# Modulation units into six places, the input projection's weights behind them in four transfers, bias lines inside its first tile

## The chip, the cores and the metric

One core of one Trainium2 chip runs the program. The metric is the device time of one execution in microseconds (us); smaller is better. Its engines are named as in the profile: PE (TensorE matmul) and PEld (its weight load), DVE (VectorE), ACT (ScalarE), POOL (GpSimd) and SP, which here only issues transfers. "SPq" and "POOLq" are the transfer queues fed by these engines. "Clock" is TensorE's granted clock, where 1.00 is 2.4 GHz and 0.50 is 1.2 GHz.

## The reference, cut to what matters

```python
def reference(...):                       # one decoder layer, prompt group (512 tokens) and 8 samples
    sh_m, sc_m, g_m, sh_f, sc_f, g_f = split(silu(c) @ w_ada + b_ada, 6)     # w_ada: 1024 x 6144
    h = rms_norm(x, norm_mix) * (1 + sc_m) + sh_m
    q, k, v, u = split(h @ w_in)                                             # w_in: 1024 x 1280
    attn = window_attention(rms(q), rms(k), v, bias=rel_bias[bucket(distance)], sinks)
    pool = pooling_mixer(u)
    x = x + g_m * (concat(attn, pool) @ w_out)
    h = rms_norm(x, norm_ffn) * (1 + sc_f) + sh_f
    return x + g_f * moe(h)               # top 4 of 32 experts, w1: 32 x 1024 x 2048, w2: 32 x 1024 x 1024
```

## The kernel before, in words

The program has two parts. `head` computes everything up to the router; `experts` streams the 32 experts' weights (402 MB in f32) through a ring of places in SBUF and multiplies with them. A barrier lies between the two. Every engine's instructions are written out by hand in program order and joined by semaphores. The change touches `head` only, nearly all of it in its first fifth.

**Modulation.** `w_ada` is cut into 24 units of 1 MB (512 rows by 512 columns). Chunk `c` of 512 outputs consists of units `2c` and `2c+1`. SP's `load_ada(n)` loads unit `n` into one of three places (`n % ADA_SLOTS`, in `m.raw`) and first waits until the unit that lay there has been used. PE's `ada(n)` multiplies it (L1349), four column groups at once. When both units of a chunk are done, DVE's `mod_row(c)` adds the bias `bada` and the four groups into `mrow` (L1025, then three times L1029). For chunks 0 to 3 (shift and scale of the mixer, units 0 to 7) PE's `turn_mod(c)` turns the row into columns (L1370). After chunk 3 DVE copies these into `modT` (L1067), forms `g1T` (L1070) and applies them to the normed and turned `hT`, one of eight row blocks `k` at a time (L1079). Chunks 4 to 11 follow between the steps of the attention.

**x.** Five row tiles (four of 128 prompt rows, one of 8 samples) are loaded by SP between the first three units, normed by ACT (L817, L821, L824), turned by PE (L1362) and copied into `hT` by ACT (L830) and DVE (L1045). PE's order is `ada(t)`, `turn_x(t)` for t = 0 to 4 (with `turn_mod(0)` before the last), `ada(5)`, `turn_mod(1)`.

**Bias lines.** For each of the eight heads a matmul of the replicated table `relrep` (33 rows, made by DVE at L1055) with `oh_line` gives a line of 383 values in all partitions (L1387). DVE copies it into `m.line` (L1061). One more matmul of 129 columns gives the samples' bias (L1389, copied at L1063). PE computes the lines after `turn_mod(1)` and before `turn_mod(2)`, `ada(6)`, `ada(7)`, `turn_mod(3)`. POOL stores the lines to HBM (`skew`) and reads them back skewed as `bias`, needed by the first scores.

**Input projection.** `w_in` (5 MB) is one transfer, which SP issues after unit 7. PE's loop over five row tiles multiplies, for each of eight `k`, 512 and 256 columns (L1435, L1436). It waits for `w_in`, for the lines, and in tile 0 for each `h_ready`. Tile t's results are normed by ACT and DVE while PE goes on with tile t+1 and then turns them (`turn_qk`). The sample tile (L1424), the four `u` blocks (L1447), the attention, output projection and router follow.

SP's queue order before is: units 0, 1, 2 each followed by an x tile, the last two x tiles, the first bias row, units 3 to 6 each when its place is free, the second bias row (after chunk 1 is added), unit 7, `w_in`, unit 8 and so on.

Of the kernel before, what the change touches and what calls it, by code (L numbers as in the profile page):

```python
# [21 lines left out]
P = 128  # L22
# [19 lines left out]
ADA_SLOTS = 3  # L42
# [83 lines left out]
def build(nc, i, o):  # L126
    m = Record()
    m.i, m.o = i, o
    with ExitStack() as ctx:
# [86 lines left out]

        m.xs = at("xs", [P, TT, D], F32, H0)
# [34 lines left out]
        m.nf = at("nf", [9, D], F32, H0 + 97792)  # L252
        m.mrow = at("mrow", [9, 2, 512], F32, H0 + 101888)
# [108 lines left out]
def head(nc, m):  # L362
# [16 lines left out]
    s.gate_step = signal("gate_step")  # L379
# [7 lines left out]
    s.win_in = signal("win_in")  # L387
# [19 lines left out]
    s.g1_ready = signal("g1_ready")  # L407
    s.hT_half = signal("hT_half")
# [17 lines left out]
    s.qn_raw = signal("qn_raw")  # L426
# [13 lines left out]
    s.spool_step = signal("spool_step")  # L440
# [24 lines left out]
    s.s_soft = signal("s_soft")  # L465
# [36 lines left out]
    ada_in = [signal(f"ada_in{n}") for n in range(ADA_SLOTS)]  # L502
# [7 lines left out]
    WHOLE = 8  # L510
    ada_bank = [bank[2 + c % 2] if c < 4 else bank[2] for c in range(CHUNKS)]
# [27 lines left out]
    with nc.Block() as block:  # L539

        @block.sync
        def _(sp):
# [7 lines left out]
            def load_ada(n):  # L550
                c, half = n // 2, n % 2
                if n >= ADA_SLOTS:
                    sp.wait_ge(s.ada_used, n - ADA_SLOTS + 1)
                src = i["w_ada"][0, half * 512:(half + 1) * 512, c * 512:(c + 1) * 512]
                sp.dma_start(m.raw[:, n % ADA_SLOTS, :].rearrange("p (k n) -> p k n", k=4),
                             src.rearrange("(k p) n -> p k n", p=P)).then_inc(ada_in[n % ADA_SLOTS], 16)

            def load_bada(q):
                sp.dma_start(m.bada[:], i["b_ada"][0:1, q * D:(q + 1) * D].to_broadcast([9, D])
                             ).then_inc(s.bada_in, 16)  # L560
# [7 lines left out]

            for n in range(ADA_SLOTS):
                load_ada(n)  # L570
                load_x(n)
            for t in range(ADA_SLOTS, TT):
                load_x(t)
            sp.wait_ge(s.c_tr, 1)
            load_bada(0)
            for n in range(ADA_SLOTS, ADA):
                load_ada(n)
                if n == 7:
                    sp.dma_start(m.w_in[:], i["w_in"][0].rearrange("(k p) n -> p k n", p=P)).then_inc(s.win_in, 16)
                if n % 4 == 2:  # L580
                    sp.wait_ge(s.mr_ready, n // 2 - 1)
                    load_bada(n // 4)
                if n in (12, 14, 16, 18):
                    if n == 12:
                        sp.wait_ge(s.z_ready, TT)
                        sp.wait_ge(s.u_ready, 4)
                    k = n - 12
                    sp.dma_start(m.w_out[:, k:k + 2, :],
                                 i["w_out"][0, k * P:(k + 2) * P, :].rearrange("(k p) n -> p k n", p=P)
                                 ).then_inc(s.wout_in, 16)  # L590
                if n >= 14 and n % 2 == 0:
                    store_mod(n // 2 - 3)
# [50 lines left out]
        def _(gp):  # L643
# [30 lines left out]
            gp.wait_ge(s.win_in, 16)  # L674
# [102 lines left out]
            gates = [0]  # L777

            def gate_step(ins):

                ins.then_inc(s.gate_step, 1)
                gates[0] += 1
                gp.wait_ge(s.gate_step, gates[0])
# [19 lines left out]
        def _(act):  # L803
# [34 lines left out]

            act.wait_ge(s.bb_in, 32)
# [162 lines left out]
        def _(v):  # L1002
# [13 lines left out]
            def mod_row(c):  # L1016

                v.wait_ge(s.ada_used, 2 * c + 2)
                v.wait_ge(s.bada_in, 16 * (c // 2 + 1))
# [5 lines left out]
                added = v.tensor_tensor(m.mrow[:, c % 2, :], ada_bank[c][0:9, :], m.bada[:, c % 2 * 512:c % 2 * 512 + 512],  # L1025
                                        ALU.add)
# [30 lines left out]
            for h in range(NH):  # L1057
                v.wait_ge(s.line_tr, h + 1)
                if not h:
                    v.wait_ge(s.c_tr, 1)  # L1060
# [9 lines left out]
            v.scalar_tensor_tensor(m.g1T[:], m.modT[:, 8:16, :], 1.0,  # L1070
                                   m.vecsT[:, 0:8].unsqueeze(2).to_broadcast([P, 8, 9]),
                                   ALU.add, ALU.mult).then_inc(s.g1_ready, 1)
            v.wait_ge(s.g1_ready, 1)
            v.wait_ge(s.xT_act, TT)
            v.wait_ge(s.xT_dve, TT)
            v.tensor_tensor(m.hT[:, :, SEQ:TOK], m.hT[:, :, SEQ:TOK], m.g1T[:, :, 0:NS],
                            ALU.mult).then_inc(s.hT_half, 1)
# [3 lines left out]
            v.wait_ge(s.hT_half, 1)  # L1081
            v.tensor_tensor(m.hT[:, :, SEQ:TOK], m.hT[:, :, SEQ:TOK], m.modT[:, 0:8, 0:NS],
                            ALU.add).then_inc(s.h_ready, 1)

# [8 lines left out]
            for t in range(TT):  # L1093
# [11 lines left out]
                if t:  # L1105
# [3 lines left out]
                                m.hrs[0:R, 0:NH].unsqueeze(2).to_broadcast([R, NH, HD]), ALU.mult).then_inc(s.qn_raw, 1)  # L1109
# [3 lines left out]
                v.wait_ge(s.qn_raw, t + 1)  # L1113
# [3 lines left out]
                v.wait_ge(s.kn_raw, 2 * t + 1)  # L1117
# [15 lines left out]
            for g, w in enumerate(WINDOWS):  # L1133
                v.tensor_reduce(m.dTs[:, g, :], m.spT[:, g, :, BUF + 1 - w:], AX_X, ALU.add).then_inc(s.spool_step, 1)
            v.wait_ge(s.spool_step, 4)
            v.wait_ge(s.Us_ready, 1)
            v.tensor_tensor(m.dTs[:], m.dTs[:], m.Us[:], ALU.add).then_inc(s.spool_step, 1)
            v.wait_ge(s.spool_step, 5)
# [81 lines left out]
            def sample_softmax():  # L1220
                v.wait_ge(s.s_tr, 1)
                v.wait_ge(s.bias64_ready, 1)
                v.scalar_tensor_tensor(m.P64[:], bank[3][0:64, 0:P], HD ** -0.5, m.bias64[:, 0:P], ALU.mult,
                                       ALU.add).then_inc(s.s_soft, 1)
                v.wait_ge(s.s_soft, 1)
                v.tensor_reduce(m.s64[:, 0:1], m.P64[:], AX_X, ALU.max).then_inc(s.s_soft, 1)
                v.wait_ge(s.s_soft, 2)
# [5 lines left out]
                v.tensor_tensor(m.s64[:, 2:3], m.s64[:, 2:3], m.s64[:, 3:4], ALU.add).then_inc(s.s_soft, 1)  # L1233
                v.wait_ge(s.s_soft, 3)
                v.reciprocal(m.s64[:, 4:5], m.s64[:, 2:3]).then_inc(s.s_soft, 1)
                v.wait_ge(s.s_soft, 4)
# [92 lines left out]
        def _(pe):  # L1329
# [10 lines left out]
            def ada(n):  # L1340

                c, half = n // 2, n % 2
                pe.wait_ge(ada_in[n % ADA_SLOTS], 16 * (n // ADA_SLOTS + 1))
# [4 lines left out]
                for k in range(4):  # L1348
                    last = mm(ada_bank[c][32 * k:32 * k + 9, :], m.cT[:, 4 * half + k, :],  # L1349
                              m.raw[:, n % ADA_SLOTS, k * 512:(k + 1) * 512], start=half == 0, stop=half == 1)  # L1350
# [38 lines left out]
            mm(bank[6][0:64, 0:P + 1], m.rel64[:].rearrange("p b h -> p (b h)"), m.oh_s[:], start=True,  # L1389
               stop=True).then_inc(s.bias64_tr, 1)  # L1390
            turn_mod(2)
            ada(6)
            ada(7)
            turn_mod(3)
# [17 lines left out]
            pe.wait_ge(s.win_in, 16)  # L1412
            pe.wait_ge(s.bias64_ready, 1)
# [1242 lines left out]
```

## Time and profile before

| | us |
|---|---|
| median of 3 runs | 1425.12 |
| lowest, highest | 1419.0, 1425.48 |
| the profiled execution | 1425.26 |
| its span in the profile | 1423.7 |
| mean granted clock | 0.92 |

| engine | busy us | share |
|---|---|---|
| PE | 1239.1 | 87% |
| DVE | 668.5 | 47% |
| ACT | 490.2 | 34% |
| POOL | 216.3 | 15% |

The program's two parts have different limits, so these shares say little of the stretch that is changed. That stretch is the first 110 us, and it is read from the timeline there.

### The profile page before, as it was taken

What the parts mean: (1) busy time and instruction counts of PE and PEld (TensorE: products, weight loads), DVE (VectorE), ACT (ScalarE), POOL (GpSimd) and SP (SyncE); (2) the same over time, 40 slices, a digit from 0 to 9 for tenths busy, and PEclk for the clock granted to TensorE, in tenths of its full rate; (3) what the DMA queues carried; (4) which work ended last, traced back from release to release, by engine and by line L of the source; (5) the groups of instructions that cost most, each with busy time, mean ns of one, the idle gap of its engine ahead of it and who ended that gap; (6) DMA issues with size and microseconds to landing.
All of it is one profiled execution on the core that took longest, in us unless ns stands there. A gap on an engine that the chain in (4) does not pass through costs nothing.

```text
span 1423.7 us, 17364 instructions
## 1 busy us (share of the span) xinstructions
PE 1239.1 (87%) x6405; PEld 729.7 (51%) x6405; DVE 668.5 (47%) x969; ACT 490.2 (34%) x703; POOL 216.3 (15%) x285
## 2 busy tenths in 40 slices
PE   5798777986899998899899969999879999999771
PEld 2353435542267564666575427556447555647330
DVE  2531562355378564353585225427334435848313
ACT  5010431231156443233464213225323333727310
POOL 2211321021101111110211102011201021101001
PEclk9799878996999999899999999999989999999975
DMA  9940585438889999999999999999999999999994
GB/s 289 383 119 5 192 286 201 173 128 324 334 309 390 375 403 397 392 396 355 376 411 406 403 391 396 395 354 405 404 388 405 367 346 408 407 410 405 413 393 187
DMA packets 113657, 481.23 MB, mean 338 GB/s; under 512 B 12497, under 2 KB 13824, under 8 KB 83820
## 3 DMA queue, kind: packets, MB, share of 16 engines
q1 hardware_dynamic: 100460, 451.52, 80.3%
q0 software_dynamic: 12768, 27.47, 7.3%
q8 instruction: 52, 0.85, 0.2%
q10 hardware_dynamic: 344, 1.12, 0.2%
q14 instruction: 33, 0.27, 0.0%
HBM read 463.46 MB, written 24.14 MB: 343 GB/s over the span
## 4 chain that ended last, share of the span: by engine, by line
PE 51%; DMA 13%; SPq 5%; DVE 5%; issue 2%; ACT 1%; POOLq 0%; DVEq 0%; ACTq 0%
PE bank L2305 49%; DMA raw<-in_w 10%; SPq L525 3%; DVE rawr L2138 1%; PE bank L2354 1%; DMA yd<-ost,slot_tok 1%; DMA yd<-gu,slot_tok 1%; SPq L531 1%; PE bank L2331 1%; ACT hi L1958 1%; SPq L535 1%; DVE gu L2102 1%; DVE gu L2100 0%; DVE yf L2298 0%; DVE yf L2295 0%
## 5 line engine op out<-in xcount | busy, mean ns | idle before, releaser
L2138 DVE TENSOR_TENSOR rawr<-raw,hi 128x1024 fp32r<-128x1024 f32 x288 | 341.2, 1220 | 137.7 <-ACT hi L1958 134.7
L1958 ACT CAST hi<-raw 128x1024 fp32r<-128x1024 f32 x288 | 295.2, 1049 | 167.0 <-PE bank L2305 117.5
L2305 PE MATMUL bank<-raw,xT_even 128*64 128x512 f32 (+1 forms) x704 | 139.5, 615 | 4.9 <-DMA raw<-in_w 4.9
L2305 PE MATMUL bank<-raw,aT 128*32 128x256 f32 (+1 forms) x992 | 116.4, 485 | 15.4 <-DMA raw<-in_w 15.4
L1853 POOL DMA_INDIRECT yd<-ost,slot_tok x31 | 54.4, 1754 | 356.3 <-ACT ost L1941 356.0
L2305 PE MATMUL bank<-raw,xT_odd 128*32 128x512 f32 (+1 forms) x544 | 88.6, 677 | 21.5 <-DMA raw<-in_w 21.5
L2305 PE MATMUL bank<-hi,xTh_even 128*128 128x512 f32 x256 | 85.1, 415 | 7.5 <-DVE rawr L2138 7.5
L2305 PE MATMUL bank<-hi,aTh 128*128 128x512 f32 x240 | 77.5, 405 | 9.7 <-DVE rawr L2138 9.7
L2305 PEld LDWEIGHTS bank<-raw,aT 128*32 128x32 f32 (+1 forms) x992 | 42.3, 126 | 79.3 <-issue 41.7
L2305 PE MATMUL bank<-rawr,xTh_even 128*128 128x512 f32 x256 | 81.7, 401 | 0.0
L2305 PE MATMUL bank<-hi,xTl_even 128*128 128x512 f32 x256 | 81.2, 399 | 0.0
L2305 PE MATMUL bank<-hi,xTh_odd 128*128 128x512 f32 x224 | 73.2, 408 | 7.0 <-DVE rawr L2138 7.0
L2305 PE MATMUL bank<-rawr,aTh 128*128 128x512 f32 x240 | 76.0, 399 | 0.0
L2305 PE MATMUL bank<-hi,aTl 128*128 128x512 f32 x240 | 75.6, 397 | 0.0
L1926 ACT ACTIVATE gu<-gu 128x512 f32<-128x512 f32 (+1 forms) x50 | 29.1, 583 | 134.9 <-DVE gu L2100 134.9
L2100 DVE TENSOR_SCALAR gu<-bank 128x512 f32<-128x512 f32 (+1 forms) x50 | 31.3, 627 | 94.0 <-PE bank L2305 94.0
L2305 PEld LDWEIGHTS bank<-raw,xT_even 128*64 128x64 f32 (+1 forms) x704 | 35.7, 128 | 69.7 <-issue 58.9
L2305 PE MATMUL bank<-rawr,xTh_odd 128*128 128x512 f32 x224 | 70.2, 395 | 0.0
L2305 PE MATMUL bank<-hi,xTl_odd 128*128 128x512 f32 x224 | 69.9, 394 | 0.0
L2156 DVE SCALAR_TENSOR_TENSOR aTl<-bank,aTh 128x512 fp32r<-128x512 f32 x30 | 20.7, 689 | 100.6 <-ACT aTh L1919 100.6
L1941 ACT ACTIVATE ost<-bank,slot_gate 128x512 f32<-128x512 f32 (+1 forms) x43 | 26.0, 633 | 120.9 <-PE bank L2305 107.6
L2089 DVE TENSOR_REDUCE slot_raw<-bank 128x1 f32<-128x2 f32 (+1 forms) x32 | 5.0, 156 | 126.4 <-PE bank L2305 125.4
(358 smaller groups left out, 1730.1 us busy)
## 6 DMA issues: line engine op xcount, KB each, us to landing
raw<-in_w SPq DMA_DIRECT2D x356, 1024.0 KB, 17.4
raw<-in_w_ada SPq DMA_DIRECT2D x24, 1024.0 KB, 6.0
raw<-in_w SPq DMA_DIRECT2D x48, 512.0 KB, 11.5
w_in_sb<-in_w_in SPq DMA_DIRECT2D x1, 5120.0 KB
w_out_sb<-in_w_out SPq DMA_DIRECT2D x4, 1024.0 KB, 6.2
early<-in_w SPq DMA_DIRECT2D x4, 1024.0 KB, 8.3
xs<-in_x_prompt SPq DMA_DIRECT2D x4, 512.0 KB, 15.7
yd<-zero POOLq DMA_DIRECT2D x4, 512.0 KB, 10.9
```

The costliest lines, as they stand in the source:

```text
L525: sp.dma_start(raw.rearrange("p (k n) -> p k n", k=2), src).then_inc(landed, 16)
L531: sp.dma_start(raw[:, kk * D:(kk + 1) * D].rearrange("p (h c) -> p h c", h=2), src[:, :, j * 512:(j + 1) * 512]).then_inc(landed, 16)
L535: sp.dma_start(raw, src).then_inc(landed, 16)
L1853: gp.indirect_dma_start(yd_of[n], bass.IndirectOffsetOnAxis(ap=m.slot_tok[:, p % 6, b:b + 1], axis=0), out_rows(p, b), None, bounds_check= ...
L1926: nc.scalar.activation(gate, gate, ACT.Silu, scale=ALPHA).then_inc(silu_ready, 1)
L1941: done = nc.scalar.activation(out_rows(p, b)[:, n * w:(n + 1) * w], src, ACT.Copy, scale=m.slot_gate[:, p % 6, b:b + 1])
L1958: nc.scalar.copy(m.hi[:, (2 * n + h) % HI, :], m.raw[:, slot, h * D:(h + 1) * D]).then_inc(hi_done, 1)
L2100: v.tensor_scalar(gate, g, LIMIT, None, ALU.min).then_inc(gmin_ready, 1)
L2102: v.tensor_scalar(up, u, LIMIT, -LIMIT, ALU.min, ALU.max).then_inc(gu_free, 1)
L2138: v.tensor_tensor(m.rawr[slot][:, half], m.raw[:, slot, half], m.hi[:, (2 * n + h) % HI, :].bitcast(F32), ALU.subtract).then_inc(lo_done, 1)
L2156: v.scalar_tensor_tensor(m.aTl[:, k:k + n, :].rearrange("p k n -> p (k n)"), bank[7][:, 0:n * P], 1.0 / ALPHA, m.aTh[:, k:k + n, :].bitcas ...
L2305: return nc.tensor.matmul(out, lhsT, rhs, start=start, stop=stop, skip_group_check=True)
```

## The change

- There are six places for modulation units. Units 0 to 5 go to places 0 to 5 (the three new ones lie in parts of SBUF that are used later); from unit 6 on the first three places are used in turn. SP issues units 0 to 4 each before its x tile, then unit 5, both bias rows (the second into a tile of its own), units 6 and 7, `w_in` in four transfers of 1.25 MB, each with its own semaphore, and unit 8.
- PE runs `ada(6)`, `turn_mod(2)`, `ada(7)`, `turn_mod(3)` right after `turn_mod(1)`. The lines are computed inside tile 0 of the projection, two before each pair of `k`, into banks 6 and 7. The samples' bias is computed before tile 1, which waits for its copy.
- DVE copies two lines after every second `k` of L1079. The two steps for the samples' part of `hT` now follow the eight `k`, and the copy of the samples' bias follows them.
- POOL waits for all four parts of `w_in` before it loads `bb`. ACT waits for chunk 3 before it writes `bb_hi`, which shares space with a new place.
- Several semaphores of DVE and POOL are merged. The four reductions for the samples' pooling now wait one for another, and `qn` and `kn` share a semaphore.

```diff
+        m.ada_more = [at(f"ada_more{n}", [P, 2048], F32, H0 + place) for n, place in enumerate((81216, 89600, 41216))]
+    def ada_place(n):
+        late = ADA_SLOTS + ADA_MORE
+        return n if n < late else (n - late) % ADA_SLOTS
...
-            for n in range(ADA_SLOTS):
-                load_ada(n)
-                load_x(n)
-            for t in range(ADA_SLOTS, TT):
+            for t in range(TT):
+                load_ada(t)
                 load_x(t)
+            load_ada(TT)
             sp.wait_ge(s.c_tr, 1)
             load_bada(0)
-            for n in range(ADA_SLOTS, ADA):
+            load_bada(1)
+            for n in range(TT + 1, WHOLE):
                 load_ada(n)
-                if n == 7:
-                    sp.dma_start(m.w_in[:], i["w_in"][0].rearrange("(k p) n -> p k n", p=P)).then_inc(s.win_in, 16)
+            for n in range(4):
+                sp.dma_start(m.w_in[:, 2 * n:2 * n + 2, :],
+                             i["w_in"][0, 2 * n * P:(2 * n + 2) * P, :].rearrange("(k p) n -> p k n", p=P)
+                             ).then_inc(win_in[n], 16)
+            for n in range(WHOLE, ADA):
+                load_ada(n)
...
+            act.wait_ge(s.ada_used, WHOLE)
+            act.wait_ge(s.mr_ready, WHOLE // 2)
             act.wait_ge(s.bb_in, 32)
...
             mod_row(2)
-            for h in range(NH):
-                v.wait_ge(s.line_tr, h + 1)
...
-                v.tensor_copy(m.line[:, h, :], bank[4 + h % 2][:, 0:LINE]).then_inc(s.line_ready, 1)
-            v.wait_ge(s.bias64_tr, 1)
-            v.tensor_copy(m.bias64[:], bank[6][0:64, 0:P + 1]).then_inc(s.bias64_ready, 1)
             mod_row(3)
...
             for k in range(KC):
                 v.tensor_scalar(m.hT[:, k, 0:SEQ], m.hT[:, k, 0:SEQ], m.g1T[:, k, 8:9], m.modT[:, k, 8:9],
                                 ALU.mult, ALU.add).then_inc(s.h_ready, 1)
+                if k % 2:
+                    for h in (k - 1, k):
+                        v.wait_ge(s.line_tr, h + 1)
+                        v.tensor_copy(m.line[:, h, :], bank[6 + h % 2][:, 0:LINE]).then_inc(s.line_ready, 1)
...
             for g, w in enumerate(WINDOWS):
-                v.tensor_reduce(m.dTs[:, g, :], m.spT[:, g, :, BUF + 1 - w:], AX_X, ALU.add).then_inc(s.spool_step, 1)
+                step(v.tensor_reduce(m.dTs[:, g, :], m.spT[:, g, :, BUF + 1 - w:], AX_X, ALU.add))
...
-            pe.wait_ge(s.rel_ready, 1)
-            for h in range(NH):
+            ada(6)
+            turn_mod(2)
+            ada(7)
+            turn_mod(3)
+            def bias_line(h):
                 if h >= 2:
                     pe.wait_ge(s.line_ready, h - 1)
-                mm(bank[4 + h % 2][:, 0:LINE], m.relrep[:, h, :], m.oh_line[:, 0:LINE], start=True,
+                mm(bank[6 + h % 2][:, 0:LINE], m.relrep[:, h, :], m.oh_line[:, 0:LINE], start=True,
                    stop=True).then_inc(s.line_tr, 1)
...
+            pe.wait_ge(s.rel_ready, 1)
+            pe.wait_ge(s.modT_ready, 1)
             for t in range(TT):
...
                 if t == 1:
-                    pe.wait_ge(s.modT_ready, 1)
+                    pe.wait_ge(s.line_ready, NH)
+                    mm(bank[6][0:64, 0:P + 1], m.rel64[:].rearrange("p b h -> p (b h)"), m.oh_s[:], start=True,
+                       stop=True).then_inc(s.bias64_tr, 1)
+                    pe.wait_ge(s.bias64_ready, 1)
...
                 for k in range(KC):
                     if not t:
+                        if not k % 2:
+                            bias_line(k)
+                            bias_line(k + 1)
+                        pe.wait_ge(win_in[k // 2], 16)
                         pe.wait_ge(s.h_ready, k + 1)
```

## Rows read from the trace of the kernel before

**Rows 1.** The page: granted clock and DMA share in tenths, 40 slices of the span.

```profile
PEclk9799878996999999899999999999989999999975
DMA  9940585438889999999999999999999999999994
```

**Rows 2.** Timeline to 58 us: start, us, engine, line, what; idle before.

```profile
4.97 1.80 SPq L548 DMA_DIRECT2D xs<-in_x_prompt  x2
...
25.86 1.06 ACT L817 ACTIVATE xn<-xs 128x1024 f32<-128x1024 f32 x1
...
16.84 7.80 SPq L555 DMA_DIRECT2D raw<-in_w_ada  x2
...
35.38 0.67 DVE L1055 COPY relrep<-relb 33x1024 f32<-33x1024 f32 x1
...
36.11 1.55 PE L1387 MATMUL bank<-oh_line_sb,relrep 33*128 33x383 f32 x4 [0.40 <-DVE relrep L1055]
...
37.93 2.12 DVE L1029 TENSOR_TENSOR mrow<-mrow,bank 9x512 f32<-9x512 f32 x3
...
43.64 0.56 DVE L1061 COPY line<-bank 128x383 f32<-128x383 f32 x1 [0.72 <-PE bank L1387]
...
48.64 0.69 PE L1389 MATMUL bank<-oh_s_sb,rel 33*64 33x129 f32 x2
...
49.37 0.28 DVE L1063 COPY bias<-bank 64x129 f32<-64x129 f32 x1
...
49.78 3.16 PE L1349 MATMUL bank<-raw,cT 128*9 128x512 f32 x16
...
53.02 0.68 DVE L1025 TENSOR_TENSOR mrow<-bank,bada 9x512 f32<-9x512 f32 x1 [3.37 <-PE bank L1349]
...
53.91 0.52 POOL L675 DMA_DIRECT2D bb<-in_b  x1 [41.85 <-DMA w_in_sb<-in_w_in]
...
56.54 0.31 DVE L1067 COPY modT<-bank 128x144 f32<-128x144 f32 x1 [0.69 <-PE bank L1370]
...
57.29 4.31 DVE L1079 TENSOR_SCALAR hT<-hT,g1T,modT 128x512 f32<-128x512 f32 x8
...
57.98 2.05 PE L1435 MATMUL bank<-w_in_sb,hT 128*128 128x512 f32 x2 [1.48 <-DVE hT L1079]
```

**Rows 3.** Timeline, tile 0's last steps and the samples' part.

```profile
69.38 1.02 PE L1435 MATMUL bank<-w_in_sb,hT 128*128 128x512 f32 x2
...
70.67 1.02 PE L1435 MATMUL bank<-w_in_sb,hT 128*128 128x512 f32 x2
...
90.71 0.52 POOL L698 DMA_DIRECT2D nf<-in_norm_ffn  x1 [4.82 <-DMA bd<-bb_lo]
...
108.25 1.14 ACT L854 COPY zs<-bank 8x320 f32<-8x320 f32 x3 [2.68 <-PE bank L1424]
...
147.32 0.56 DVE L1134 TENSOR_REDUCE dTs<-spT 128x8 f32<-128x8 f32 x4
```

**Rows 4.** By stretch: busy us of PE, PEld, DVE, ACT, POOL; clock, DMA share, GB/s.

```profile
38.60:52.20 13.60, 11.51 (x30) 4.84 (x34) 6.02 (x12) 0.00 (x0) 0.00 (x0) 0.50 1.03 417
...
55.80:62.50 6.70, 5.11 (x11) 2.81 (x12) 5.18 (x13) 1.49 (x1) 6.46 (x10) 0.50 1.04 351
62.50:70.70 8.20, 8.20 (x28) 4.97 (x27) 3.35 (x1) 1.26 (x1) 0.00 (x0) 0.99 1.16 442
...
345.00:1423.00 1078.00, 968.06 (x5138) 581.72 (x5134) 518.57 (x657) 400.85 (x487) 146.12 (x157) 0.94 0.98 381
```

**Rows 5.** The same view and columns, within 26 to 36 us.

```profile
26.00:28.00 2.00, 1.89 (x12) 1.59 (x15) 1.76 (x4) 1.44 (x4) 0.00 (x0) 1.00 1.04 384
...
34.00:36.00 2.00, 1.04 (x12) 0.32 (x4) 1.94 (x4) 0.00 (x0) 0.00 (x0) 1.00 0.28 101
```

**Rows 6.** Transfers by their issue, alone in their windows: KB, us to landing.

```profile
xs<-in_x_prompt SPq DMA_DIRECT2D x1, 512.0 KB, 18.2
...
raw<-in_w_ada SPq DMA_DIRECT2D x1, 1024.0 KB, 8.4
```

More of the change, by code:

```diff
@@ L386, in head @@
     s.bb_in = signal("bb_in")
-    s.win_in = signal("win_in")
+    win_in = [signal(f"win_in{n}") for n in range(4)]
     s.wout_in = signal("wout_in")
@@ L501, in head @@
     x_in = [signal(f"x_in{t}") for t in range(TT)]
-    ada_in = [signal(f"ada_in{n}") for n in range(ADA_SLOTS)]
+    ada_in = [signal(f"ada_in{n}") for n in range(ADA_SLOTS + ADA_MORE)]
     h2_free = [signal(f"h2_free{n}") for n in range(2)]
@@ L510, in head, with ada_unit, ada_landed @@
     WHOLE = 8
+    def ada_place(n):
+        late = ADA_SLOTS + ADA_MORE
+        return n if n < late else (n - late) % ADA_SLOTS
+    def ada_unit(n):
+        a = ada_place(n)
+        return m.raw[:, a, :] if a < ADA_SLOTS else m.ada_more[a - ADA_SLOTS][:]
+    def ada_landed(n):
+        return 16 * (1 + sum(ada_place(k) == ada_place(n) for k in range(n)))
     ada_bank = [bank[2 + c % 2] if c < 4 else bank[2] for c in range(CHUNKS)]
@@ L551, in load_ada @@
                 c, half = n // 2, n % 2
-                if n >= ADA_SLOTS:
-                    sp.wait_ge(s.ada_used, n - ADA_SLOTS + 1)
+                earlier = [k for k in range(n) if ada_place(k) == ada_place(n)]
+                if earlier:
+                    sp.wait_ge(s.ada_used, earlier[-1] + 1)
                 src = i["w_ada"][0, half * 512:(half + 1) * 512, c * 512:(c + 1) * 512]
-                sp.dma_start(m.raw[:, n % ADA_SLOTS, :].rearrange("p (k n) -> p k n", k=4),
-                             src.rearrange("(k p) n -> p k n", p=P)).then_inc(ada_in[n % ADA_SLOTS], 16)
+                sp.dma_start(ada_unit(n).rearrange("p (k n) -> p k n", k=4),
+                             src.rearrange("(k p) n -> p k n", p=P)).then_inc(ada_in[ada_place(n)], 16)
             def load_bada(q):
-                sp.dma_start(m.bada[:], i["b_ada"][0:1, q * D:(q + 1) * D].to_broadcast([9, D])
+                sp.dma_start((m.bada_1 if q == 1 else m.bada)[:], i["b_ada"][0:1, q * D:(q + 1) * D].to_broadcast([9, D])
                              ).then_inc(s.bada_in, 16)
@@ L673, in _ @@
                 gp.memset(m.found[:, :, t, 1], float(P * t - FAR)).then_inc(s.zeros_ready, 1)
-            gp.wait_ge(s.win_in, 16)
+            for n in range(4):
+                gp.wait_ge(win_in[n], 16)
             gp.dma_start(m.bb[:, 0:2 * D], i["b1"][0]).then_inc(s.bb_in, 16)
@@ L1018, in mod_row @@
                 v.wait_ge(s.ada_used, 2 * c + 2)
-                v.wait_ge(s.bada_in, 16 * (c // 2 + 1))
+                v.wait_ge(s.bada_in, 16 * max(c // 2 + 1, 2))
+                shift = (m.bada_1 if c // 2 == 1 else m.bada)[:, c % 2 * 512:c % 2 * 512 + 512]
                 if c >= 2:
@@ L1024, in mod_row @@
                         v.wait_ge(s.mod_out, 16 * (c - 5))
-                added = v.tensor_tensor(m.mrow[:, c % 2, :], ada_bank[c][0:9, :], m.bada[:, c % 2 * 512:c % 2 * 512 + 512],
-                                        ALU.add)
+                added = v.tensor_tensor(m.mrow[:, c % 2, :], ada_bank[c][0:9, :], shift, ALU.add)
                 for q in range(1, 4):
@@ L1069, in _ @@
             v.wait_ge(s.vecs_ready, 1)
[L1070 to L1073, printed above, removed]
+            step(v.scalar_tensor_tensor(m.g1T[:], m.modT[:, 8:16, :], 1.0,
+                                        m.vecsT[:, 0:8].unsqueeze(2).to_broadcast([P, 8, 9]), ALU.add, ALU.mult))
             v.wait_ge(s.xT_act, TT)
             v.wait_ge(s.xT_dve, TT)
-            v.tensor_tensor(m.hT[:, :, SEQ:TOK], m.hT[:, :, SEQ:TOK], m.g1T[:, :, 0:NS],
-                            ALU.mult).then_inc(s.hT_half, 1)
             for k in range(KC):
@@ L1232, in sample_softmax @@
                 v.wait_ge(s.s_exp, 2)
[L1233 to L1236, printed above, removed]
+                step(v.tensor_tensor(m.s64[:, 2:3], m.s64[:, 2:3], m.s64[:, 3:4], ALU.add))
+                step(v.reciprocal(m.s64[:, 4:5], m.s64[:, 2:3]))
                 v.tensor_scalar(m.P64[:], m.P64[:], m.s64[:, 4:5], None, ALU.mult).then_inc(s.s_norm, 1)
```

50 lines of the change are left out of this document (16 added, 34 removed).

## The prediction

> **What bounds the kernel now.** I read the page first. The transfers are busy at 0.9 or more in every slice from 320 us on, and they are idle for stretches before that [rows 1]. In the expert stage the transfers run at a share of 0.98 and 381 GB/s [rows 4]. None of its transfers is issued before the head has got far, so whatever the head gains or loses should move that stage as a block. The change lies in the first 110 us, so the timeline there decides.
>
> In that timeline the reader should follow one chain [rows 2]. With chunk 1 of the modulation added, DVE makes `relrep` at 35.38, and PE starts the eight bias lines at 36.11. `mod_row(2)` ends at 40.05 beside them. PE is with lines and the samples' bias until 49.3 (48.64 + 0.69), though, and only then turns chunk 2 and multiplies units 6 and 7 (49.78 to 52.94). `mod_row(3)` starts at 53.02, `modT` is there at 56.85, and the projection starts at 57.98. `w_in` landed at 53.9, where POOL's wait for it ends, so it isn't what tile 0 waits for: the lines are. From 57.98 PE has work without a gap until the sample tile.
>
> The clock is half of this story [rows 4]. From 38.6 to 52.2 it is at 0.50 (1.2 GHz), although PE is busy 11.51 of the 13.60 us, most of it with lines. Tile 0 starts at 0.50 and returns to 1.00 at 62.5, after 4.5 us of its full-height matmuls.
>
> **The change, part by part.**
>
> *The units' transfers.* In the queue two more units lie ahead of x's last full tile and of the samples' rows than before, one ahead of each. A full x tile of the pair issued from 4.97 on took 18.2 us to land [rows 6]; the last was issued near 5.9 [rows 2], so it landed near 24.1. One more 1 MB unit ahead of it, at the 384 GB/s of that stretch [rows 5], is 2.7 us, so it lands near 27. ACT takes tile 3 up at 25.86, without a wait [rows 2]. What is late next is ACT's norm of tile 3 by 1.1 us and then `turn_x(3)` and `turn_x(4)` on PE; I carry +1.0 us to `relrep`, which starts at 36.4 then. The floor is 0 (the slack takes it), the ceiling 2.8. Unit 5 was issued near 24.3 (the last 0.37 of 16.84 + 7.80) and landed 8.4 us later, at 32.7 [rows 6]. The same bytes lie ahead of it now, so it lands there again. Units 6 and 7 follow without the pause of 34 to 36 us (101 GB/s, [rows 5]): 2.8 us each, 35.5 and 38.3. Four parts of `w_in`, 1.31 MB each at 417 GB/s [rows 4], land near 41.5, 44.6, 47.8 and 51. Unit 8, not needed before the attention, pays for it.
>
> *The lines leave the chain.* After 36.4: `relrep` 0.67, `mod_row(2)` 2.83 (53.02 to 53.73 + 2.12), ending at 39.9. That was hidden under lines; now it is bare. `ada(6)` lies beside it, for its unit has landed. `turn_mod(2)` takes 0.45 (49.33 to 49.78), `ada(7)` at most 1.6 (3.16 for two, mostly at half clock, [rows 2]), so `mod_row(3)` starts at 41.9. From there to `modT` took 3.83 us (53.02 to 56.85), so it is there at 45.7, against 56.85: 11.1 us earlier.
>
> *The lines come back in tile 0.* One `k` takes 1.29 us at full clock (69.38 to 70.67, [rows 3]), eight take 10.3. A line at half clock takes 1.28 (0.56 of copy and 0.72 of wait, [rows 2], one of six such copies), so 0.64 at full, eight 5.1. Together 15.4 us of full-clock work. With H us of it spent at half clock, tile 0 lasts 15.4 + H/2. Before, H was 4.5. Now each pair of `k` at half clock (5.1 us) is cut off by two lines (2.6 us), and lines alone did not bring the clock back from 41 to 49 us. The lower end for H is 0 (the clock is still full when tile 0 starts), the upper one for a likely course the whole 13.6 us stretch of [rows 4]. I take 7.4: lines first (2.6), then nearly one pair of `k`, like the 4.5 of before. Loss 3.7, so tile 0 ends at 45.7 + 15.4 + 3.7 = 64.8, against 70.67.
>
> Nothing else should hold it. DVE has two `k` at 0.54 (4.31 for eight, [rows 2]) and two copies at 0.56 for a pair, 2.2 us against PE's 3.9, and `w_in`'s parts are there: the last is needed after 58 and lands near 51.
>
> *Before tile 1.* The samples' bias matmul (0.2 at full clock), its copy (0.28, [rows 2]) and two semaphore hops stand bare: 0.8 us. Tile 1 starts at 65.6 instead of 70.67: 5.1 us gained. DVE's `bb_lo` (3.35 us, the DVE time of 62.5 to 70.7, [rows 4]) now runs when tile 0's norms are wanted. These have 10.3 us of tile 1 as cover, and need about 7 with it. Without that cover it would cost 3.
>
> *Moved waits on POOL and ACT.* `skew` leaves when line 8 is copied, near 60, about when it left before. `bd` lands and frees POOL at 90.7, while ACT needs it for the samples at 108.25 [rows 3], now near 103. There are still some 12 us between. ACT's new wait for chunk 3 ends near 45, before `bb` arrives. Nothing is charged. The places of later units are as before.
>
> *Merged semaphores.* The four reductions took 0.56 us together [rows 3]; waiting one for another, and `kn` before `qn`'s second step in the sample tile, costs 0.3. The others have as many waits as before: 0.
>
> **Sum.** 5.1 - 0.3 = 4.8 us gained. The profiled execution took 1425.26 (1.6 us over its span), which is at the median of 1425.12, so 1420.5 us, 0.3% below. The three runs spread over 6.5 us.
>
> A rule on H, apart from the sum: the Trainium skill (TensorE: Matmul & The Clock Gate, "What you observe") says that the full clock comes about 4 us into sustained matmul activity. If lines count as such, H would be about 4 and the estimate 1418.8. The trace here doesn't bear that out for lines.
>
> **Rivals.**
>
> *The clock returns early, or never falls.* H as in tile 0 before, 4.5, gives 1.4 us more: 1419.0. With H = 0 and `ada(7)` at full clock it is 1416.3. For it: `ada(6)` and `ada(7)` come sooner, and 52.2 shows the clock rising under such units. Against: before tile 0 PE rests most of 4 us for `mod_row(3)`, and the clock fell in the same rest before (from 55.8 it is 0.50, [rows 4]). This is also where the skill's rule of the paragraph above would lead.
>
> *The gain melts.* The x tiles come the full 2.8 us late down to `modT` (1.8 lost), or the lines hold the clock for 13.6 us (3.1 lost), or both: 1422.3 to 1425.4. That is also "it does nothing": what the lines cost inside the tile is what they cost ahead of it.
>
> *Slower: lines hold the clock at half for all of tile 0.* Then it lasts 30.8 us and ends at 76.5, and the bias before tile 1 takes 1.1: 7.2 us lost, 1432.5. It decides from H = 17 on, where the gain is nil. For it: 38.6 to 52.2. Against: five full-height microseconds lie between the lines, more than the 4.5 that sufficed.
>
> *A later stage answers.* The head's attention and router stages shift against the clock's falls and rises. One fall more or less costs or gives 1 to 3 us and could carry the result past 7 us of gain.
>
> **How the numbers follow.** My forecast 0.42, clock early 0.24, melted 0.20, lines hold it 0.06, later stage 0.08. What a measurement of this kernel can tell from no change is about 0.5%, 7.1 us. Faster by more: most of the early-clock case with the runs' scatter (0.18), a part of mine (0.09) and half of the later stage: 0.31. Slower by more: 0.05. Within: 0.64. The range from 1412 takes in the early clock with 4 us of scatter, to 1427 the melted case with 2.
>
> **What would show it.** `modT` copied near 45.7 (42 to 48); first line right behind it; last `k` of tile 0 at 64 to 66; `w_in`'s last part before 52; tile 1 under 1 us behind tile 0; everything from 110 on earlier by one amount. It is wrong if ACT waits for x beyond 28, if tile 0 lasts over 22 us, or if PE waits for `w_in` or for `line` copies inside it.

## The result, and the profile after

The changed kernel takes 1428.39 us (median of 20 runs, 1422.21 to 1435.49) against 1420.66 for the kernel before beside it (20 runs): a ratio of 1.0053, interval 1.0035 to 1.0071. It is slower by 0.5%, by about 7.5 us. I had forecast 1420.5 us and 4.8 us faster, with a range to 1427. The profiled execution has a span of 1428.0 us against 1423.7. A ratio, here and below, leaves out runs over 1.5% above the fastest of their kernel: one run of the kernel before at 2043.74 us, and the two longest of the twelve of `e9_lines_spread`.

The page of the changed kernel, granted clock and DMA share; they answer to [rows 1]:

```profile
PEclk9699877996899999899999999999979999999775
DMA  9940385438989999999999999999999999999995
```

The later stages look alike, so the head has to tell the difference. Its timeline in the changed kernel; columns as in [rows 2]:

```profile
7.50 9.58 SPq L557 DMA_DIRECT2D xs<-in_x_prompt  x1
...
22.25 3.35 SPq L569 DMA_DIRECT2D bada<-in_b_ada  x2
...
20.29 1.06 ACT L832 ACTIVATE xn<-xs 128x1024 f32<-128x1024 f32 x1 [7.03 <-DMA xs<-in_x_prompt]
...
29.19 1.06 ACT L832 ACTIVATE xn<-xs 128x1024 f32<-128x1024 f32 x1 [1.15 <-DMA xs<-in_x_prompt]
...
36.16 0.68 DVE L1043 TENSOR_TENSOR mrow<-bank,bada 9x512 f32<-9x512 f32 x1 [9.18 <-DMA bada<-in_b_ada]
...
39.10 1.15 ACT L839 ACTIVATE xn<-xs,rstd 128x1024 f32<-128x1024 f32 x1 [8.43 <-DVE rstd L1059]
...
40.86 1.94 PE L1367 MATMUL bank<-ident,xn 128*128 128x128 f32 x8 [8.91 <-ACT hT L845]
...
43.45 0.67 DVE L1043 TENSOR_TENSOR mrow<-bank,bada 9x512 f32<-9x512 f32 x1
...
46.41 0.68 DVE L1072 COPY relrep<-relb 33x1024 f32<-33x1024 f32 x1
...
52.25 0.68 DVE L1043 TENSOR_TENSOR mrow<-bank,bada 9x512 f32<-9x512 f32 x1 [1.51 <-PE bank L1354]
...
54.66 0.52 POOL L690 DMA_DIRECT2D bb<-in_b  x1 [42.62 <-DMA w_in_sb<-in_w_in]
...
55.77 0.31 DVE L1077 COPY modT<-bank 128x144 f32<-128x144 f32 x1 [0.69 <-PE bank L1375]
...
56.22 2.89 PE L1397 MATMUL bank<-oh_line_sb,relrep 33*128 33x383 f32 x4 [0.49 <-DVE modT L1077]
...
68.14 1.55 PE L1397 MATMUL bank<-oh_line_sb,relrep 33*128 33x383 f32 x4
...
72.40 1.55 PE L1397 MATMUL bank<-oh_line_sb,relrep 33*128 33x383 f32 x4
...
76.66 0.43 PE L1422 MATMUL bank<-oh_s_sb,rel 33*64 33x129 f32 x2
...
77.47 1.13 PE L1446 MATMUL bank<-w_in_sb,hT 128*128 128x512 f32 x2 [0.38 <-DVE bias L1095]
```

The line to look at is the one at 36.16. It is DVE's first add of chunk 0, and DVE had stood 9.18 us for the bias row `bada`. In the kernel before, the same add needs no wait; its timeline, same columns:

```profile
8.93 1.35 SPq L559 DMA_DIRECT2D bada<-in_b_ada  x1
...
24.93 0.68 DVE L1025 TENSOR_TENSOR mrow<-bank,bada 9x512 f32<-9x512 f32 x1
```

There the row is issued at 8.93, behind three units and all of x. In the changed kernel SP issues both rows between 22.25 and 25.60, behind six units and all of x. SP came there late, too: it stood 9.58 us on the issue of x tile 3 (7.50 to 17.08) alone. `mod_row(c)` now waits for `16 * max(c // 2 + 1, 2)`, so that chunk 0 needs both rows. They had landed at 36.1.

DVE works in order, and behind chunk 0 in its list stand the norms of tiles 3 and 4. ACT was through with its first step of tile 3 by 30.7 and then waited 8.43 us for `rstd`; PE waited 8.91 us for the tile to turn. Then four chunks follow each other. `relrep` comes at 46.41 (35.38 in [rows 2]), `modT` is copied at 55.77 (56.54), though the eight lines are gone from before it. The lines are then paid in tile 0, and tile 1 starts at 77.47 instead of 70.67.

By stretches of the changed kernel; columns as in [rows 4]:

```profile
36.00:49.60 13.60, 8.74 (x48) 3.80 (x48) 9.38 (x17) 4.75 (x8) 0.00 (x0) 0.50 1.02 411
49.80:53.00 3.20, 1.54 (x16) 0.44 (x12) 1.62 (x4) 0.00 (x0) 0.00 (x0) 1.00 1.04 389
...
55.80:63.10 7.30, 6.88 (x10) 3.35 (x11) 3.67 (x8) 0.00 (x0) 4.01 (x8) 0.50 1.04 310
63.10:77.40 14.30, 13.99 (x41) 6.70 (x39) 5.79 (x14) 3.39 (x3) 2.56 (x3) 1.00 0.49 199
345.00:1423.00 1078.00, 976.93 (x5152) 584.94 (x5152) 524.58 (x664) 401.45 (x488) 146.70 (x163) 0.93 0.98 381
```

Tile 0 begins at the half clock and is back at 1.00 at 63.1: 6.9 us at half where I had taken 7.4. The expert stage moves the same 381 GB/s at the same share of 0.98 as in [rows 4], so the head's loss is carried through.

### The profile page after: what moved, and what is told of

Its sections match the earlier page's. It is cut to its first block, busy times and chain, and to the rows that moved or that the text cites. A ratio compares the mean times of both kernels' runs of the same rounds, so it can differ in the third digit from the quotient of the medians.

```text
span 1428.0 us, 17377 instructions
## 1 busy us (share of the span) xinstructions
PE 1246.5 (87%) x6405; PEld 731.9 (51%) x6405; DVE 669.4 (47%) x969; ACT 490.3 (34%) x703; POOL 214.1 (15%) x285
## 4 chain that ended last, share of the span: by engine, by line
PE 52%; DMA 12%; SPq 6%; DVE 4%; issue 2%; ACT 1%; POOLq 0%; ACTq 0%; DVEq 0%
PE bank L2316 50%; DMA raw<-in_w 9%; SPq L534 3%; DMA yd<-ost,slot_tok 1%; DVE rawr L2149 1%; PE bank L2365 1%; SPq L544 1%; DMA yd<-gu,slot_tok 1%; PE bank L2342 1%; SPq L540 1%; ACT hi L1969 1%; DVE gu L2113 1%; DMA yf<-yd 0%; DVE gu L2111 0%; DVE yf L2306 0%
## 5 line engine op out<-in xcount | busy, mean ns | idle before, releaser
L2316 PE MATMUL bank<-raw,aT 128*32 128x256 f32 (+1 forms) x992 | 119.3, 495 | 13.3 <-DMA raw<-in_w 13.2
## 6 DMA issues: line engine op xcount, KB each, us to landing
raw<-in_w SPq DMA_DIRECT2D x48, 512.0 KB, 11.9
```

What stands on the lines that cost most here:

```text
L2316: return nc.tensor.matmul(out, lhsT, rhs, start=start, stop=stop, skip_group_check=True)
```

## The experiments

My theory after the result: the bias rows' place in SP's queue costs some 7 us, the units ahead of x another 2 or 3, and the forecast mechanism, the lines taken off the chain to `modT`, is sound beneath both. The rivals: that chunk 0 waits for two rows instead of one; that it is the place of the norms on DVE; that the lines cost too much inside the tile; that the four transfers of `w_in` or the six places do harm.

Landmarks in us from the start of each profiled execution (tile 0 starts with its first line or `k`), and times. The kernel before ran beside every set: its median was 1422.71 us beside e1 to e4, 1422.39 beside e5 to e8 and 1424.33 beside e9 and e10. A ratio is not the quotient of the two medians and differs from it by up to 0.15%.

```
kernel                modT copied  tile 1  tile 0 starts  time (runs), ratio [interval]
before                   56.54     70.67     57.98        1420.66 (20)
changed                  55.77     77.47     56.22        1428.39 (20), 1.0053 [1.0035, 1.0071]
e1_rows_early            48.54     70.65     48.99        1418.44 (12), 0.9975 [0.9951, 0.9998]
e2_own_waits             54.26     75.93     54.71        1424.81 (1)
e3_norm_first            53.64     74.64     54.09        1430.39 (1)
e4_before_late_row       65.54     80.07     66.98        1429.08 (10), 1.0044 [1.0017, 1.0071]
e5_three_places          45.70     67.73     46.16        1418.66 (12), 0.9960 [0.9933, 0.9988]
e6_x_first               46.48     68.54     46.93        1418.56 (12), 0.9962 [0.9939, 0.9985]
e7_one_w_in              45.71     71.14     46.17        1419.95 (1)
e8_lines_in_gaps         52.45     66.29     53.76        1416.36 (12), 0.9944 [0.9918, 0.9969]
e9_lines_spread          52.66     68.60     56.02        1416.80 (12), 0.9934 [0.9907, 0.9961]
e10_lines_block          45.08     70.17     45.54        1428.36 (1)
```

A single time says little here: the kernel before alone spread over 10 us or more in every set of runs. Where there is one, the landmarks carry the verdict. Landmarks scatter too, for each stands for one execution. `e6_x_first`, `e7_one_w_in` and `e10_lines_block` have the same order up to `modT`, and it is copied at 46.48, 45.71 and 45.08. In the three with the changed kernel's queue (changed, e2, e3) x tile 1 is taken up at 20.29, 18.29 and 18.41. A difference in a landmark of under some 2 us is not read as an effect of an edit, unless it is taken from a nearer event.

**Both rows ahead of unit 3** (`e1_rows_early`).

```
             for t in range(TT):
+                if t == 3:
+                    sp.wait_ge(s.c_tr, 1)
+                    load_bada(0)
+                    load_bada(1)
                 load_ada(t)
                 load_x(t)
             load_ada(TT)
-            sp.wait_ge(s.c_tr, 1)
-            load_bada(0)
-            load_bada(1)
```

> Changed kernel, but both bias rows of the first four chunks are issued ahead of unit 3. Theory A (DVE's chunk 0 waits for the second bias row, and everything behind it on DVE with it): the wait of 9.2 us ahead of chunk 0's add is gone, modT is copied at 46 to 48 us instead of 55.8, tile 1 of the projection starts at 67 to 69 instead of 77.5, and the time is 8 to 10 us below that of the changed kernel, at or a little below the kernel before. Theory B (the x tiles that land about 3 us late behind more units set the delay): the wait is gone but modT comes only 2 to 4 us earlier, at 52 or later.

Its timeline:

```profile
6.01 2.19 SPq L569 DMA_DIRECT2D bada<-in_b_ada  x2
...
9.29 7.15 SPq L557 DMA_DIRECT2D xs<-in_x_prompt  x1
...
27.96 0.67 DVE L1044 TENSOR_TENSOR mrow<-bank,bada 9x512 f32<-9x512 f32 x1
...
30.70 1.06 ACT L833 ACTIVATE xn<-xs 128x1024 f32<-128x1024 f32 x1 [1.58 <-DMA xs<-in_x_prompt]
...
48.54 0.31 DVE L1078 COPY modT<-bank 128x144 f32<-128x144 f32 x1 [0.69 <-PE bank L1376]
```

The wait for `bada` is gone and chunk 0 starts at 27.96, not 36.16. `modT` comes 7.2 us earlier and tile 1 6.8 us earlier; the time goes from 0.5% above the kernel before to 0.25% below. SP still stands 7.15 us on the issue of x tile 3, so that standing alone is not the cost. `modT` and tile 1 are a little later than theory A had them (48 and 69 at the latest), but far from theory B. What is left is in ACT's line: x tile 3 comes at 30.70.

**A semaphore of its own for the second row** (`e2_own_waits`); the order of the issues stays.

```
...
-                v.wait_ge(s.bada_in, 16 * max(c // 2 + 1, 2))
+                if c // 2 == 1:
+                    v.wait_ge(s.bada_in1, 16)
+                else:
+                    v.wait_ge(s.bada_in, 16 * max(c // 2, 1))
```

> Changed kernel, order of transfers kept, but the second bias row has a semaphore of its own, so that chunks 0 and 1 wait for the first row alone. Theory A': it is the demand for both rows that costs: chunk 0 is added near 25 to 28 us, modT near 46 to 48. Theory A'': it is the place of both rows behind five units and four x tiles: the first row lands 1 to 3 us before the second, chunk 0 starts at 33 to 35 instead of 36.2, modT at 53 to 55.

Its timeline:

```profile
34.65 0.68 DVE L1047 TENSOR_TENSOR mrow<-bank,bada 9x512 f32<-9x512 f32 x1 [8.78 <-DMA bada<-in_b_ada]
```

Chunk 0 and `modT` come 1.5 us earlier than in the changed kernel, but SP also reached the rows 0.9 us earlier (21.34 against 22.25), which the edit does not touch. Counted from the start of their issue, the first row alone is there after 13.3 us, both rows after 13.9 us in the changed kernel and 13.8 in the next one (21.11 to 34.90). The doubled threshold is thus worth some 0.5 us, and the place in the queue is the large part.

**Norms of tiles 3 and 4 ahead of chunk 0 on DVE** (`e3_norm_first`).

```
-                if t in (2, TP):
-                    mod_row(t // 2 - 1)
+                if t == TP:
+                    mod_row(0)
             v.wait_ge(s.x_tr, 2 * TT)
...
+            mod_row(1)
```

> Changed kernel, order of transfers kept, but DVE takes chunk 0 behind the norms of tiles 3 and 4 instead of ahead of them. This leaves the late row and takes away what is queued behind it. If the blocked norms are the larger part, ACT no longer waits 8.4 us for DVE, tile 3 is turned near 31 us instead of 40.9 and modT comes at 49 to 51 us; if the late row alone sets the pace, through four chunks of 2.8 us in a row on DVE, modT stays at 54 to 56.

Its timeline:

```profile
28.95 0.16 DVE L1059 RECIPROCAL rstd<-rstd 128x1 f32<-128x1 f32 x1 [3.25 <-ACT rstd L836]
...
34.90 0.68 DVE L1043 TENSOR_TENSOR mrow<-bank,bada 9x512 f32<-9x512 f32 x1 [1.84 <-DMA bada<-in_b_ada]
```

Both norms now run beside the wait, which shrinks to 1.84 us, but chunk 0 still starts only at 34.90. `modT` is at 53.64: 2.1 us gained, between my two expectations. Of these, 1.3 are the row itself, which was there earlier in this execution with the same queue. From chunk 0 to `modT` it is 18.7 us against 19.6, so the norms' place is worth 0.9. I had put more on the blocked norms than this. Four chunks of 2.8 us, with the turns and units between them, follow the late row whatever stands ahead of it, so the row sets the pace and the norms in its shadow are a side effect.

**The late row put into the kernel before** (`e4_before_late_row`): its one row is issued behind unit 5.

```
-            load_bada(0)
             for n in range(ADA_SLOTS, ADA):
                 load_ada(n)
+                if n == TT:
+                    load_bada(0)
```

> Kernel before with one edit: its first bias row is issued behind unit 5 instead of ahead of unit 3. Theory A: the row lands after 30 us, DVE stands in front of chunk 0 from 24.9 on, the first k of the projection starts 5 to 9 us after the 57.98 of before, and the time is 5 to 9 us longer. Theory B: chunk 0 has slack (its turn on PE comes at 32.7), under 2 us.

Its timeline:

```profile
33.89 0.68 DVE L1026 TENSOR_TENSOR mrow<-bank,bada 9x512 f32<-9x512 f32 x1 [8.34 <-DMA bada<-in_b_ada]
...
44.87 2.70 PE L1388 MATMUL bank<-oh_line_sb,relrep 33*128 33x383 f32 x4 [0.40 <-DVE relrep L1056]
```

With nothing else of the change in it, the kernel before gets the same stall of 8.34 us. The lines begin at 44.87 against 36.11 in [rows 2], the first `k` comes at 66.98 against 57.98, and the time is 1429.08 us (10 runs) against 1422.71: 1.0044, interval 1.0017 to 1.0071. (The landmarks are from the longest of these ten runs, 1438.64 us.) This step alone is enough to make what was measured.

**x and both rows ahead of the further units**, with six places (`e6_x_first`) and with three (`e5_three_places`, where `ADA_MORE` is 0 besides).

```
-            for t in range(TT):
+            for t in range(3):
                 load_ada(t)
                 load_x(t)
-            load_ada(TT)
+            for t in range(3, TT):
+                load_x(t)
             sp.wait_ge(s.c_tr, 1)
             load_bada(0)
             load_bada(1)
-            for n in range(TT + 1, WHOLE):
+            for n in range(3, WHOLE):
                 load_ada(n)
```

> Changed kernel with six places, but x tiles and both bias rows ahead of units 3, 4 and 5. Theory A: x lands as in before, 3 us earlier than in the changed kernel; modT at 44.5 to 47, tile 1 at 66 to 68, 3 to 5 us below before, no different from three places within 1 us. If units already in the queue slow x wherever they stand, x lands 2 to 3 us late again and modT stays at 48.

> Lines in tile 0 and w_in in four parts behind unit 7, but three places, the x tiles and both bias rows ahead of unit 3 as in the kernel before. Theory A (the order of lines is the only gain, the six places only hurt the arrival of x and rows): x tiles land as in before (17.0, 22.6, near 24), modT at 45 to 47 us, tile 1 starts at 66.5 to 68.5 against 70.7 before and 70.65 with the rows alone moved, time 3 to 5 us below before. Theory B (the places are needed, because unit 7 and w_in come late with three): PE waits for unit 7 or for w_in, modT at 49 or later or a wait for w_in of over 2 us in tile 0, time as before.

Timeline of the one with six places:

```profile
26.17 0.68 DVE L1044 TENSOR_TENSOR mrow<-bank,bada 9x512 f32<-9x512 f32 x1 [0.16 <-DMA bada<-in_b_ada]
...
35.76 0.68 DVE L1073 COPY relrep<-relb 33x1024 f32<-33x1024 f32 x1
...
42.97 0.68 DVE L1044 TENSOR_TENSOR mrow<-bank,bada 9x512 f32<-9x512 f32 x1 [3.79 <-PE bank L1355]
...
49.75 2.07 PE L1447 MATMUL bank<-w_in_sb,hT 128*128 128x512 f32 x2
```

`modT` comes at 46.48 and 45.70, another 2.1 and 2.8 us below the version with the early rows alone; e7 and e10, with the same order up to there, have it 2.8 and 3.5 below. So two units ahead of x cost some 2 to 3 us; a single execution with the early rows alone does not size it more closely. These are the times at which I had forecast `modT`. Both versions beat the kernel before by 0.4%. They cannot be told apart (1418.56 and 1418.66), so the three further places bring nothing here that shows.

**`w_in` in one transfer again** (`e7_one_w_in`, from the version with six places and x first).

```
...
-            for n in range(4):
-                sp.dma_start(m.w_in[:, 2 * n:2 * n + 2, :],
-                             i["w_in"][0, 2 * n * P:(2 * n + 2) * P, :].rearrange("(k p) n -> p k n", p=P)
-                             ).then_inc(win_in[n], 16)
+            sp.dma_start(m.w_in[:], i["w_in"][0].rearrange("(k p) n -> p k n", p=P)).then_inc(win_in[0], 16)
```

> As the kernel with x and rows first, but w_in in one transfer. The parts of w_in land from 41 on and the last near 51; tile 0 wants the first near 48. So the first k should wait until 51 to 54 and modT be unchanged: tile 1 starts 2 to 5 us later than with four parts. If w_in is there anyway by then, no difference.

Its timeline:

```profile
53.11 2.07 PE L1443 MATMUL bank<-w_in_sb,hT 128*128 128x512 f32 x2 [4.05 <-DMA w_in_sb<-in_w_in]
```

Once `modT` is early, PE stands 4.05 us before the first `k` until all of `w_in` has landed at 53.1. The first `k` is 3.4 us later and tile 1 2.6 us later. The four parts are needed, but by the traces only in a version without the late rows: in the changed kernel the first `k` comes at 59.0, and all four parts had landed by 54.66.

**Lines in the gaps ahead of `modT`** (`e8_lines_in_gaps`, same base): three behind unit 6, five behind unit 7, ACT copies them, and tile 0 is free of them.

```
...
             ada(6)
+            pe.wait_ge(s.rel_ready, 1)
+            for h in range(3):
+                bias_line(h)
             turn_mod(2)
             ada(7)
+            for h in range(3, NH):
+                bias_line(h)
+            mm(bank[6][0:64, 0:P + 1], m.rel64[:].rearrange("p b h -> p (b h)"), m.oh_s[:], start=True,
+               stop=True).then_inc(s.bias64_tr, 1)
             turn_mod(3)
```

> As the kernel with x and rows first, but the lines stand in PE's two waits for DVE (three behind unit 6, five behind unit 7) and ACT copies them instead of DVE, so that tile 0 is free of them. Theory L (lines inside tile 0 cost their own time, 5.1 us at full clock, and 0.4 a pair in switches): modT at 46 to 49 (five lines at half clock last 6.4 us, twice the wait they stand in), tile 0 lasts 12.5 to 13.5 us, tile 1 starts at 61 to 64, the time is 3 to 5 us below that with the lines in tile 0. Theory C (what counts is when the clock returns): the lines in the gaps change no more than 2 us.

Its timeline:

```profile
44.53 6.75 PE L1392 MATMUL bank<-oh_line_sb,relrep 33*128 33x383 f32 x10
...
52.45 0.31 DVE L1083 COPY modT<-bank 128x144 f32<-128x144 f32 x1 [4.96 <-PE bank L1375]
...
66.49 0.60 ACT L890 ACTIVATE sq<-bank 128x512 f32<-128x512 f32 x1 [0.90 <-PE bank L1447]
```

Five lines behind unit 7 are too many: at the half clock they take 6.75 us, and `modT` waits 4.96 us for the turn behind them. It comes at 52.45, where I had expected 46 to 49, and tile 1 starts at 66.29, where I had expected 61 to 64; that is still 2.2 us before the woven version `e6_x_first`, whose lines stand inside tile 0. The time is the lowest so far at 0.9944, interval 0.9918 to 0.9969; it overlaps with that of `e6_x_first`, so that it beats the kernel before is shown, that it beats the woven version is not.

**Lines spread more finely, three places** (`e9_lines_spread`): three lines behind unit 6, one ahead of unit 7, two behind it, two behind the last turn. The edit is shown against the version just before.

```
...
             turn_mod(2)
+            bias_line(3)
             ada(7)
-            for h in range(3, NH):
-                bias_line(h)
-            mm(bank[6][0:64, 0:P + 1], m.rel64[:].rearrange("p b h -> p (b h)"), m.oh_s[:], start=True,
-               stop=True).then_inc(s.bias64_tr, 1)
+            bias_line(4)
+            bias_line(5)
             turn_mod(3)
+            bias_line(6)
+            bias_line(7)
+            mm(bank[2][0:64, 0:P + 1], m.rel64[:].rearrange("p b h -> p (b h)"), m.oh_s[:], start=True,
+               stop=True).then_inc(s.bias64_tr, 1)
```

> Three places, x and rows first, lines copied by ACT and spread over PE's waits: three behind unit 6, one ahead of unit 7, two behind it, two behind the last turn. In the kernel with lines in the gaps DVE stood 5.0 us for modT behind five lines at half clock (6.4 us in a wait of 3). With two there (2.6 us) modT should come at 45.5 to 48 us instead of 52.5; the two behind the turn cost 1 to 2 us before the first k. Tile 0 free of lines then lasts 12.5 to 13.5 us: tile 1 starts at 61 to 64, time 1414 to 1417. If the clock decides, tile 0 takes longer by what modT gains, and tile 1 starts at 65 or later.

1416.8 us (12 runs) against 1424.33: 0.9934, interval 0.9907 to 0.9961. Over all twelve runs the quotient of the means is 0.9947, so that it is better than the last is not shown. Its profiled execution is the longest of the twelve (1425.33 us), so I read its head with caution: `modT` is at 52.66 there, where I had expected 45.5 to 48, no earlier than with five lines in a block. The clock is at 0.50 there from 36 us on, and the four lines that stand ahead of unit 7 push it to 47.19, against 42.70 in `e8_lines_in_gaps`. Spreading the lines moved the delay and did not remove it.

**All lines as one block between `modT` and tile 0** (`e10_lines_block`, from `e6_x_first`).

```
...
             pe.wait_ge(s.modT_ready, 1)
+            for h in range(NH):
+                bias_line(h)
...
-                        if not k % 2:
-                            bias_line(k)
-                            bias_line(k + 1)
```

> As the kernel with six places, x and rows first, but all eight lines as one block between modT and the first k. Theory C (lines hold the clock at half, the full-height matmuls bring it back): the block runs at half clock, 10 to 11 us, tile 0 behind it has 4 to 6 us at half clock, tile 1 starts at 70.5 to 73 instead of 68.5. If lines bring the clock back as any matmul does, the block takes under 8 us and tile 1 starts at 67 to 69.

Its timeline, and its stretches:

```profile
45.54 10.55 PE L1398 MATMUL bank<-oh_line_sb,relrep 33*128 33x383 f32 x16 [0.49 <-DVE modT L1078]
```

```profile
45.60:56.00 10.40, 10.40 (x16) 4.78 (x16) 7.53 (x16) 0.00 (x0) 3.18 (x7) 0.50 1.03 395
56.00:61.40 5.40, 5.40 (x10) 2.96 (x10) 0.91 (x3) 1.45 (x1) 4.69 (x7) 0.50 1.04 341
61.40:70.00 8.60, 8.39 (x27) 4.61 (x25) 0.17 (x1) 1.83 (x3) 0.00 (x0) 0.98 1.08 403
```

PE is busy for 10.40 of 10.40 us with lines and the clock stays at 0.50 throughout. It returns only 5.4 us into the full-height matmuls of tile 0. `modT` is copied 1.4 us earlier than in the woven version (the scatter of equal heads), yet tile 1 starts 1.6 later: from `modT` to tile 1 woven lines are worth 3.0 us. The sum closes to 0.1: the clock is at 0.50 for 15.9 us after `modT` here and for 7.3 there (46.93 to 54.2, six of the eight lines behind that), which is 4.3 us, less 1.2 for the three further changes between lines and `k` of the woven order (0.4 each, below). `e8_lines_in_gaps` agrees that lines do not hold the full clock: it falls from 1.00 to 0.50 at 41.0 while PE is busy without a gap with lines that began at 39.31. The rule of the Trainium skill that I had set beside the forecast (TensorE: Matmul & The Clock Gate, "What you observe": full clock about 4 us into sustained matmul activity) is contradicted by this row if 33-row matmuls count as such; for the full-height ones it is nearly met with 5.4.

## Why the prediction was wrong, point by point

**The step that failed** is "I carry +1.0 us to `relrep`, which starts at 36.4 then". It started at 46.41, 10.0 us later. In that step I moved x behind two more units and followed x alone. The two bias rows, which SP issues behind the same units, had no line in the working: DVE's wait for them, 9.18 us, was put at nothing without a reason. Of the 10.0 us, 7.4 are the rows (46.41 against 39.05 with the rows early), shown by `e1_rows_early` and, in the kernel before, by `e4_before_late_row`. The other 2.6 are x and scatter: 39.05 is 3.7 behind [rows 2], where I had taken 1.0 with a ceiling of 2.8. Tile 3 was to land near 27 and came at 29.19, or 30.70 with the rows early, but at 27.6 and 27.4 in e2 and e3, whose queues are that of the changed kernel. Tile 1, with nothing more ahead of it than before, was 3.3 us late already (20.29 against 16.98, timeline of each). That is not shown to be an effect of the change: `e4_before_late_row` has tile 1 at 18.32 with the queue of the kernel before up to there, and of all the traces here the one of the kernel before has it earliest. My base was one early execution. One of my own signs of being wrong showed itself: ACT waited for x until 29.19, beyond 28.

**From `relrep` to `modT`** I had 9.3 us (36.4 to 45.7, the end of the copy); measured were 9.7 (46.41 to 56.08). With x and the rows first `modT`'s copy ended at 46.8 and 46.0. The mechanism, lines off the chain, was right. One term beneath it was too low: unit 7 was to land at 38.3, and in `e6_x_first` PE waited for it until 41.00. In the changed kernel the late rows hid this.

**Tile 0** was to last 19.1 us, 15.4 of work and 3.7 for the clock. It lasted 20.4 (56.22 to 76.66). The clock's part was right: 6.9 us at half cost 3.45. The work was 17.0: a pair of `k` with its two lines takes 4.26 us at full clock (68.14 to 72.40), not the 3.86 that I summed. The parts had their right size: two lines in a row at full clock end 0.65 us apart (copies at 40.25 and 40.90 in `e8_lines_in_gaps`, 0.64 taken), and a `k` among others takes 1.29. Between lines the two `k` take 1.39 each, and two lines take 1.48 up to the next `k`, not 1.28. So the 0.4 us a pair, 1.6 in all, come where the shape changes; why was not tried.

**Before tile 1**: 0.81 us (76.66 to 77.47), forecast 0.8.

**The sum** closes: tile 1 was forecast at 65.6 and came 11.9 later. That is 10.4 for `modT`, 0.1 for the hop to the first line and 1.3 for the tile.

**`w_in`** did not bind, as forecast, and its wait on POOL ended at 54.66 instead of 51. What the split is worth I had not priced: nothing in the changed kernel, 3.4 us of the first `k` with x and the rows first (`e7_one_w_in`).

**The rivals.** The slower one named the wrong mechanism: it decides from 17 us at the half clock on, and 6.9 came. "The gain melts" is what x did, but that is at most 2.6 us of 10. The clock neither returned early nor stayed down. The range missed because a wait was missing in it; sizes alone, corrected, would have left the time inside.

**What stays open.** The head's shift and the end agree only to some 3 us. The changed kernel is 6.8 us late at tile 1 and 7.5 at the end; `e1_rows_early` is level at tile 1 and 3.6 us ahead at the end (0.9975 of 1422.71); `e6_x_first` is 2.1 ahead and 5.4 at the end. Some 3 us are gained behind the head where the late rows are gone. `e4_before_late_row`, which has none of the merged semaphores, is 9.4 us late at tile 1 and 6.3 at the end, so they do not explain it there. A part may be no gain at all: every shift is taken from the one trace of the kernel before, whose x tile 1 was there 0.8 to 3.3 us earlier than in any other trace. What the clock's later falls add was not tried.

## What to carry to other kernels

When transfers are put ahead in a queue, list every small transfer that stands behind them and the first instruction that waits for it: here 36 KB issued 13 us late (22.25 against 8.93) stopped an in-order engine for 9 us, and everything behind it. Read each changed wait threshold for what it asks of the first iteration, and give more buffers to big loads only behind the small ones that are needed first. A piece of work taken off one chain is worth what the next wait leaves of it: the version with x and the rows first got the forecast `modT`, and only there was the split of `w_in` of use. And take the landmarks of more than one execution before a shift of 1 or 2 us is built on: equal heads differed by that much here.

## What the runs showed of the hardware

SP can stand long on one issue. In the changed kernel the issue of a 512 KB tile took 9.58 us, in `e1_rows_early` 7.15; the longest of an x tile or a bias row in the kernel before was 2.08. What stands behind such an issue in the program waits with it, however small it is.

A small transfer does not overtake. The Trainium skill says (DMA: Bandwidth & Descriptors, "Queues, rings and completion order") that each engine consumes a ring's descriptors in order. The rows agree: the two rows of 36 KB, issued from 22.25 to 25.60 behind the units, were there at 36.1. They came later than that rule alone asks: in windows of 4 us the changed kernel moves 226 to 394 GB/s there, so the 8.4 MB of units and x ahead of them should have been through between 30 and 32 (an estimate from those rates). The remaining 4 to 6 us are not explained. The early rows of `e6_x_first` show the same lag: with 5.3 MB ahead, which should have been through near 22 by the same count, they were there at 26.17.

A transfer's landing scatters from one execution to the next. x tile 1 is taken up between 16.98 and 20.29 in the twelve traces. Among the kernels with equal queues up to there it is 18.29, 18.41 and 20.29 (e2, e3, changed) and 17.81 to 19.20 (e6, e7, e8, e10).

Matmuls of 33 rows did not bring the full clock back: in `e10_lines_block` eight lines in a row kept PE busy for 10.40 of 10.40 us at 0.50. The full-height ones behind them had it back after 5.4 us, those of the kernel before after 4.5 [rows 4].
